# Attention: values product as high and low parts with channel-major output, probabilities divided ahead of their transposes

## The reference

```python
s = jnp.einsum('brnqhd,brnkhd->brnhqk', qb, kw).astype(jnp.float32)
s = s + bias.transpose(2, 0, 1)
...
m = jnp.max(s, axis=-1, keepdims=True)
p = jnp.exp(s - m)
den = jnp.sum(p, axis=-1, keepdims=True)
o = jnp.einsum('brnhqk,brnkhd->brnqhd', (p / den).astype(v.dtype), vw)
...
w = jax.nn.softmax(jnp.stack(lses, axis=0), axis=0)
return jnp.einsum('ibsh,ibshd->bshd', w.astype(q.dtype), jnp.stack(outs, axis=0))
...
mix = jnp.concatenate([attn, sgu], axis=-1) @ w_out
```

## Time and profile before

| | us |
|---|---|
| median of 3 runs | 1803.13 (1801.1 to 1805.96) |
| the profiled execution, time | 1803.39 |
| its span, first to last instruction | 1801.6 |
| PE busy | 1771.5 (98%) |
| DVE, ACT, POOL busy | 817.6, 652.3, 731.4 |
| attention's pairs, from the first transposes of v to the rest of the output projection | 73.3 to 221.0 |

### The profile page before, as it was taken

How to read it: one execution, slowest core, us unless ns; L and a number is a source line. 1 busy time by engine, 2 the same in 40 slices (tenths; PEclk the granted TensorE clock), 3 DMA queues, 4 the chain that set the end, 5 groups by cost and what they waited for, 6 DMA issues and landing times.

```text
span 1801.6 us, 24039 instructions
## 1 busy us (share of the span) xinstructions
PE 1771.5 (98%) x8280; PEld 1447.6 (80%) x8280; DVE 817.6 (45%) x1443; ACT 652.3 (36%) x933; POOL 731.4 (41%) x322
## 2 busy tenths in 40 slices
PE   8999999999999999999999999999999999999998
PEld 7788877888888788788888888788887788888886
DVE  4644566333333596522242244566665432422425
ACT  5544444222222333632222233454544432222323
POOL 3222235444445378244444343342423444443441
PEclk9999999999999999999999999999999999999999
DMA  8341123323222242233323233221212233232221
GB/s 221 86 99 57 47 71 105 96 97 99 94 93 94 71 123 83 70 94 117 93 82 105 93 96 102 71 83 58 82 58 70 83 105 94 82 105 93 94 92 47
DMA packets 153686, 162.28 MB, mean 90 GB/s; under 512 B 10627, under 2 KB 114679, under 8 KB 153631
## 3 DMA queue, kind: packets, MB, share of 16 engines
q1 hardware_dynamic: 149167, 158.66, 28.8%
q10 hardware_dynamic: 4464, 2.89, 0.5%
HBM read 157.84 MB, written 3.67 MB: 90 GB/s over the span
## 4 chain that ended last, share of the span: by engine, by line
PE 55%; issue 29%; POOL 10%; DVE 3%; ACT 1%; POOLq 0%; DVEq 0%; ACTq 0%
PE ps L1167 50%; POOL wlo L604 10%; PE ps L1341 2%; PE ps L1479 1%; PE ps L1330 1%; DVE ss L1697 1%; DVE acc L1719 1%; DVE h_lo L1685 0%; PE ps L1305 0%; PE ps L1306 0%; POOL wlo L611 0%; DVE xT L1722 0%; DVE sq L1878 0%; DVE xT L2187 0%; PE ps L1289 0%
## 5 line engine op out<-in xcount | busy, mean ns | idle before, releaser
L604 POOL TENSOR_TENSOR wlo<-raw,whi 128x1024 fp32r<-128x1024 f32 x256 | 617.3, 2426 | 961.2 <-ACT whi L680 947.6
L1167 PE MATMUL ps<-h_hi,wlo 128*128 128x512 f32 x1472 | 589.1, 400 | 6.3 <-POOL wlo L604 4.2
L1167 PE MATMUL ps<-h_hi,whi 128*128 128x512 f32 x1472 | 576.0, 391 | 0.0
L1167 PE MATMUL ps<-h_lo,whi 128*128 128x512 f32 x1472 | 574.9, 391 | 0.0
L680 ACT ACTIVATE whi<-raw 128x1024 fp32r<-128x1024 f32 x282 | 292.0, 1054 | 502.1 <-PE ps L1167 501.6
L1167 PEld LDWEIGHTS ps<-h_hi,wlo 128*128 128x128 f32 x1472 | 277.2, 188 | 66.6 <-issue 4.9
L1167 PE MATMUL ps<-m_hi,wlo 128*128 128x512 f32 x800 | 321.2, 401 | 3.4 <-POOL wlo L611 1.9
L1167 PEld LDWEIGHTS ps<-h_hi,whi 128*128 128x128 f32 x1472 | 276.8, 188 | 59.3
L1167 PEld LDWEIGHTS ps<-h_lo,whi 128*128 128x128 f32 x1472 | 277.4, 188 | 58.2 <-issue 3.1
L1167 PE MATMUL ps<-m_lo,whi 128*128 128x512 f32 x800 | 317.7, 397 | 0.0
L1167 PE MATMUL ps<-m_hi,whi 128*128 128x512 f32 x800 | 317.7, 397 | 0.0
(11 more groups left out here) (263 smaller groups left out, 1428.6 us busy)
## 6 DMA issues: line engine op xcount, KB each, us to landing
raw<-in_ffn_w SPq DMA_DIRECT2D x264, 256.0 KB, 2.9
raw<-in_w_ff SPq DMA_DIRECT2D x128, 256.0 KB, 2.9
raw<-in_hg_w_in SPq DMA_DIRECT2D x64, 256.0 KB, 3.2
raw<-in_w_in SPq DMA_DIRECT2D x40, 256.0 KB, 3.8
raw<-in_cp_w_in SPq DMA_DIRECT2D x24, 256.0 KB, 3.0
raw<-in_w_out SPq DMA_DIRECT2D x16, 256.0 KB, 2.9
raw<-in_cp_w_out SPq DMA_DIRECT2D x16, 256.0 KB, 3.0
raw<-in_hg_w_out SPq DMA_DIRECT2D x16, 256.0 KB, 2.9
```

Of the source, the lines that this page charges most:

```text
L604: pool.tensor_tensor(wlo[:, u % RING, :, :], raw[:, u % RING, :, :], whi[:, u % RING, :, :].bitcast(F32), ALU.subtract).then_inc(unit_lo, 1)
L1167: mm = pe.matmul(ps[:, b, :], wt[:, s, a, m * P:(m + 1) * P], xt[:, kts[a], :], start=starts and a == 0 and i == 0, stop=last)
```

## The change

The values product takes the same high and low form as the dense ones, with its output channel-major. Each block is divided by its sum in place before it is turned (DVE `scaled_weights`: a reciprocal on 128x1 and a product on 128x512). ACT makes `prob_hi` from bank 6 (`high`), DVE `prob_lo` (`turned_low`), which frees bank 6. v of a head is stationary as 128 columns: its 64 high columns and its 64 low ones (`vtok`, ACT and DVE `values_low`), and a head takes 8 matmuls of 512 columns (4 key tiles, low and high of the probabilities). The half of the output partitions that comes from v's low part is moved to the other half by ACT (`o_across`), added by DVE (`o_total`), and split by ACT `o_high` and DVE `o_low`. `onorm` and its transposes go. `values(1)` of a pair runs behind the first dense tiles of the next, and so does the transposing of v. ACT's drains of the next q and k are split by head, with `high(6)` and `high(7)` between and behind. `cuts` tells how many dense tiles stand between the steps.

```diff
+            def o_across(e, p):
+                act.wait_ge(filled[7], nth("att", ("o", e), p))
+                act.activation(o_other[own_rows(e), :], ps[own_rows(1 - e), 7, :], ACT.Copy).then_inc(o_moved, 1)
+
+            def o_high(e, p):
+                act.wait_ge(drained[7], nth("att", ("o", e), p))
+                act.activation(head_row(m_hi, e, p), head_row(osum, e, p), ACT.Copy).then_inc(o_hi, 1)
...
+                def high(i):
+                    cols = slice((i % 4) * P, (i % 4 + 1) * P)
+                    act.wait_ge(filled[6], nth("att", ("t", i), p))
+                    act.activation(prob_hi[:, :, cols], ps[:, 6, :].rearrange("p (k q) -> p k q", q=P), ACT.Copy)\
+                        .then_inc(turn_hi, 1)
...
+                high(0)
                 units(0)
-                if before_it is not None:
-                    pair_out(before_it)
-                weights(2)
                 act.wait_ge(u_cubed, 2 * p + 2)
                 act.activation(u_in[:, :], u_in[:, :], ACT.Tanh, scale=GELU_SCALE).then_inc(u_tanh, 1)
+                weights(2)
+                high(1)
...
+            def values(e, p):
+
+                pe.wait_ge(drained[6], nth("att", ("t", 4 * e + 3), p))
+                pe.wait_ge(drained[7], before("att", ("o", e), p))
+                for k in range(TT):
+                    pe.matmul(ps[:, 7, :], vtok[:, k, e, :], prob_lo[:, k, :], start=k == 0, stop=False)
+                    mm = pe.matmul(ps[:, 7, :], vtok[:, k, e, :], prob_hi[:, k, :], start=False, stop=k == TT - 1)
                 mm.then_inc(filled[7], 1)
 
-            def attend(p, units, before_it, following=None):
+            def attend(p, piece, before_it, following=None, cuts=(0, 2, 5, 7, 9, 11, 13, 15, 17, 20, 22, 24, 26, 28, 30, 32)):
...
                 def turn(i):
-                    pe.wait_ge(prob_ready, p * 8 + (i + 1))
+                    pe.wait_ge(prob_scaled, p * 8 + (i + 1))
                     pe.wait_ge(drained[6], before("att", ("t", i), p))
...
+            def scaled_weights(i, p):
+                dve.wait_ge(prob_ready, p * 8 + (i + 1))
+                dve.reciprocal(rden[:, i:i + 1], den[:, i:i + 1]).then_inc(den_inv, 1)
+                dve.wait_ge(den_inv, p * 8 + (i + 1))
+                dve.tensor_scalar(prob[:, i % 2, :], prob[:, i % 2, :], rden[:, i:i + 1], None, ALU.mult)\
+                    .then_inc(prob_scaled, 1)
+
+            def turned_low(i, p):
+                cols = slice((i % 4) * P, (i % 4 + 1) * P)
+                dve.wait_ge(turn_hi, p * 8 + (i + 1))
+                dve.tensor_tensor(prob_lo[:, :, cols], ps[:, 6, :].rearrange("p (k q) -> p k q", q=P),
+                                  prob_hi[:, :, cols].bitcast(F32), ALU.subtract).then_inc(drained[6], 1)
```

More of the change, by code:

```diff
@@ L819, in attend @@
                 act.activation(tile_of(m_hi, 4 + p), ug[:, :], ACT.Copy).then_inc(sg_hi, 1)
+                high(2)
                 units(1)
[L821 to L824, removed]
-                if following is not None:
-                    drain_qkv("qkv", following, following + 1)
+                weights(4)
+                high(3)
+                weights(5)
+                o_across(0, p)
+                units(2)
+                high(4)
+                o_high(0, p)
+                weights(6)
+                high(5)
+                units(3)
+                weights(7)
+                if following is not None:
+                    drain_head("qkv", following, following + 1, 0)
+                high(6)
+                if following is not None:
+                    drain_head("qkv", following, following + 1, 1)
+                    drain_values("qkv", following)
+                high(7)
             u_first = nth("qkv0", ("m", 3))
@@ L832, in _ @@
             attend(PAIRS - 1, u_first + PAIRS - 1, lambda i: split(U_WOUT, i) if i < 3 else None, PAIRS - 2)
-            pair_out(PAIRS - 1)
+            o_across(1, PAIRS - 1)
+            o_high(1, PAIRS - 1)
             act.preload_act_table_set(LOG_TABLES)
@@ L1331, in turn @@
                     mm.then_inc(filled[6], 1)
[L1333 to L1345, removed]
@@ L1362, in attend @@
[L1362 to L1368, removed]
+                dense(0)
+                if before_it is not None:
+                    values(1, before_it)
+                values_turned(p)
+                dense(1)
+                for i in range(4):
+                    turn(i)
+                    dense(2 + 2 * i)
+                    scores(i + 2, p)
+                    if i < 3:
+                        dense(3 + 2 * i)
@@ L1369, in attend @@
+                values(0, p)
+                dense(9)
                 turn(4)
-                units(2, second)
+                dense(10)
                 scores(6, p)
+                dense(11)
                 turn(5)
-                units(2, third)
+                dense(12)
                 scores(7, p)
-                units(3, slice(0, 6))
-                values(4)
-                values(5)
+                dense(13)
                 turn(6)
-                units(3, third)
+                dense(14)
@@ L1908, in attend @@
                 biased(2, p)
                 u_cube(p)
-                turned(1)
+                if p:
+                    o_low(1, p - 1)
+                scaled_weights(2, p)
+                turned_low(1, p)
                 biased(3, p)
                 sgu_out(p)
-                if p:
-                    pair_low(p - 1)
+                scaled_weights(3, p)
+                turned_low(2, p)
+                biased(4, p)
                 sgu_low(p)
-                turned(2)
-                biased(4, p)
@@ L1918, in attend @@
-                turned(3)
+                scaled_weights(4, p)
+                turned_low(3, p)
                 biased(5, p)
-                normal(0, p)
-                turned(4)
+                scaled_weights(5, p)
+                o_total(0, p)
+                turned_low(4, p)
                 biased(6, p)
-                turned(5)
+                o_low(0, p)
+                scaled_weights(6, p)
+                turned_low(5, p)
                 biased(7, p)
@@ L1945, in _ @@
                 attend(p)
-            pair_low(PAIRS - 1)
+            o_total(1, PAIRS - 1)
+            o_low(1, PAIRS - 1)
             logits = [vecs[:, COL["hg_lb_logits_2"] + i * HG_HEADS:COL["hg_lb_logits_2"] + (i + 1) * HG_HEADS]
```

159 lines of the change are left out of this document (81 added, 78 removed).

## The result

The changed kernel takes 1817.78 us (median of 4, 1817.66 to 1821.81), the kernel before beside it 1804.55 (1801.1 to 1806.06). The ratio is 1.0081, with a 95% interval of 1.006 to 1.0103: slower, by 13.2 us or 0.8%. The profiled execution took 1817.76 us, 14.4 more than that of before (1803.39).

A forecast was written before the change was run, and what follows sets the result against it. PE, busy 98% of the span, was taken to bound the kernel. Pairs followed through the queues sum to 157.8 us; with 2.1 and 1 more, 160.9 against 147.7 before: +13.2, so 1816 us, range 1801 to 1821.

The forecast's parts named there:

- PE's own work: PE in the attention's pairs: values matmuls and onorm transposes exchanged, 3.6 us less a pair, 14.6 in four, leaving 33.7.
- ACT and DVE: Added work in a pair: ACT +6.6 to 24.5 us, DVE +6.4 to 25.7, neither full beside PE's 33.7.
- The pair's end: PE waits before scores(0), turn(7) and the next pair's first dense tile: 0.6, 0.7 and 1.2, together 2.5 us a pair.
- POOL's hold: POOL's wlo holds DVE's u_cube and sgu_low 2.0 us each; PE waits before turn(2), turn(3), values(0): 3.7 us a pair.
- The sum: Pairs walked through the three queues: 37.1, 39.8, 39.8, 41.1; 157.8 us, with 3.1 for branches and restarts 160.9, +13.2.
- Elsewhere nothing: Outside the attention nothing moves; ACT's table load, pushed behind PE's last zv tile, is taken up by ACT's idle time.
- Not held: Rival: DVE's products and sgu_low pass beside POOL or miss it; attention 147.3 us, -0.4, kernel 1803; chance 0.20.
- All hidden: Rival: ACT and DVE run far enough ahead that all PE waits are hidden; -14.6, 1789; chance 0.06.
- The clock (1820): Rival: PE's clock falls behind the last pair's waits of 3.5 and 2.9 us; +2 to 4, 1820; chance 0.12.

The follow-up runs named there:

- the last kernel: Changed kernel with ACT's and DVE's queues and PE's cuts ordered anew, in the second order (u_cube behind scaled_weights(0), weight units later in a pair): 1788.17 us, ratio 0.9906.
- the swap of two operations: Changed kernel with ACT draining the next pair's first head ahead of the exp of block 7 instead of behind it: 1815.42 us, ratio 1.0068.
- the kernel that kept the clock up: Changed kernel with twelve small matmuls of 128 columns into unused bank 7 ahead of turn(2) of every pair: 1819.4 us, ratio 1.0084.
- the kernel with three moves: Changed kernel with u_cube ahead of turned_low(0), sgu_low behind scaled_weights(5), drain_head(0) of the next pair ahead of exp(7): 1804.67 us, ratio 0.9999.
- the kernel with POOL cut short: Changed kernel with POOL's wlo on 8 of 512 columns for 16 weight units of the attention, the other low parts left out: 1804.87 us, ratio 1.0011.
- two moves: Changed kernel with u_cube ahead of turned_low(0) and sgu_low behind scaled_weights(5), drain_head left in place: 1808.64 us, ratio 1.0025.
- the first reordered kernel: Changed kernel's operations with ACT's and DVE's queues and PE's cuts ordered anew, u_cube ahead of turned_low(0), sgu_low behind biased(7): 1797.83 us, ratio 0.9954.
- the kernel with one hold undone: Changed kernel with DVE's u_cube of each pair moved ahead of turned_low(0): 1813.55 us, ratio 1.0065.

## Why the prediction was right

It said 1816 us, +13; measured are 1817.8 and +13.2. By its steps:

- **PE's own work** (-14.6 us, 33.7 a pair). Right, and a little small. In the last kernel, where nearly every wait is gone, a pair of the loop takes 33.5 us, 4.4 less than the 37.87 for which PE was busy before, where 3.6 were forecast; the attention takes 15.4 less than before (15.8 with the transposes of v).
- **ACT and DVE.** `high` 0.589 against 0.60. The product was mis-sized: 0.487 us, not the 0.42 of the earlier trace rows, whose factor is a constant where this one is read from SBUF (whether that is the reason wasn't tried); 8 x 0.07 = 0.5 us a pair on DVE.
- **The pair's end** (0.6 + 0.7 + 1.2 = 2.5). Measured 0.62 + 0.51 + 1.17 = 2.3, and the swap of two operations changed just these.
- **POOL's hold** (1.8 before turn(2), 0.35 before turn(3), 1.5 before values(0)). The mechanism was right in every pair but the sizes were not: 2.34, 0 and 0.17. The sum of waits is 2.5 instead of 3.7, because the clock fell, which the prediction gave as a rival for the last pair alone. Some eight matmuls at 0.43 instead of 0.23 are 1.6 us more of PE work in the place of the second and third wait. In the kernel that kept the clock up the second is under 0.1, the third 1.23 and the pair as long. With the 2.34 before turn(2) that is 3.6 us, the sum that was forecast, but out of errors of 0.5, 0.3 and 0.3 that cancel: luck. The first was 0.5 us too short mainly by where PE stands. Counted from h, the start of `high(0)` at 118.47, POOL's operation runs from 1.76 to 4.17 (forecast 1.64 to 4.02) and turn(2) starts at 7.92 (7.8), but PE is there at 5.58 instead of 6.0. That `u_cube` starts 0.27 us into `wlo`, not 0.42, costs nothing, since it ends with POOL's operation either way.
- **The sum.** Pairs of 37.7, 41.1, 41.2 and 41.9 us, where the walk had 37.1, 39.8, 39.8 and 41.1, and 3.1 on top. Their sum is 161.9 against 160.9. The 3.1 had to be 4.1; in the kernel with three moves a pair of the loop takes 37.3 us with 2.66 us of waits in four places, so it takes 0.9 us beyond its 33.7 and these waits: about 0.24 us a restart. That is an estimate, but the rows point the same way: behind a wait the next matmul starts 0.34 us after the first (110.68 and 111.02 in the changed kernel), not 0.23, and the last one before it counts its full 0.40. The last pair's waits were 3.34, none, 1.99, 0.48, 1.64 and 1.38 (forecast 3.5, 1.0, 2.9, 0.75, 1.8, 1.5), again with the fallen clock in the place of the missing ones.
- **Elsewhere nothing.** Right: 1580.7 against 1580.6 us behind the attention.
- **The rivals.** Not held (1803) is near what the kernel with POOL cut short does, 1804.87, though its attention took 150.5 us and not 147.3; 1.5 of the difference is the fallen clock, and the rest wasn't followed up. The 148.9 named there follows from none of its terms; they add up to 144.2, on which its time rests. The margin of 0.4 us that was given for the hold was enough. All hidden (1789) is not what this change does, but another order of the same operations gives 1788. The argument against it, that the pair's end can't cover 7.5 us of queue, held for the order of the change only. The clock (1820) fell, in three pairs, and cost next to nothing: 161.7 us of attention with the clock kept up, against 161.9. The estimate of +2 to 4 overlooked how much of the fall is taken up by waits that would stand there anyway. Where no such wait follows, a fall did cost: 1.5 us with POOL cut short, about 1.4 with two moves.

The Trainium skill (SBUF — State Buffer, SBUF: two separate sides) calls the pair of ports that VectorE and GpSimd share an exclusive lock, on which the loser blocks fully, not a share of bandwidth. The runs agree: wherever it starts inside POOL's operation, a product ends 0.28 us behind it and the subtraction of `sgu_low` 0.55 behind it (0.42 or 0.49, and 0.69, alone). It also says that the one that starts first gets the lock. In the first reordered kernel a product that starts 0.20 us ahead of POOL takes its usual 0.48, and POOL's operation 2.55 instead of 2.40, which agrees. But the trace has the product at 130.01, POOL at 130.02, and the product waiting; a distance of 0.01 us decides nothing.

## What to carry to other kernels

Put every VectorE pass that works on SBUF alone where GpSimd is idle, or ahead of it, and count a near miss as a hit; the cheap place to look is a 0.4 us operation that takes 2.4. When a change adds work to engines that have room, follow their strict queues at the two or three places where PE is short of cover: here the loss was in the places of three operations, not in the amount of new work. A change that takes work from the bounding engine may need the whole order and the cuts made anew before the gain shows.

## What the runs showed of the hardware beyond that

Waits of the same length were followed by a fall of the clock in one place and not in another. It was at the lower level for 3.4 us or more behind each wait of 2.34 us and more before turn(2), and not behind the 1.41 us in the kernel before. Behind a wait of 2.54 us before values(0) of the last pair it fell in the kernel with one hold undone, and not in the one with the small matmuls. With POOL cut short it fell behind the 1.11 us at the end of pair 0, in the others with the same wait there it did not. So the length of the wait alone doesn't tell. A wait of 1.64 us before turn(7) of the last pair was followed by it in two kernels (the pair's end, two moves) and not in the others that have it, such as the one with three moves, in whose window at the same place the clock is 1.00:

```profile
216.80:220.20 3.40, 3.39 (x16) 2.55 (x17) 0.69 (x1) 0.60 (x1) 0.00 (x0) 1.00 0.02 5
```

DVE's operations that read PSUM ran inside POOL's `wlo` at their usual time, and so did those on one column (timelines of the first reordered kernel; POOL's operation runs from 125.83 to 128.38, and the product at 125.63 is the one that started ahead of it):

```profile
125.83 2.55 POOL L631 TENSOR_TENSOR wlo<-raw,whi 128x1024 fp32r<-128x1024 f32 x1 [4.87 <-ACT whi L707]
...
125.63 0.48 DVE L1909 TENSOR_SCALAR sq<-sq,rden 128x512 f32<-128x512 f32 x1
126.03 0.68 DVE L1938 CUSTOM_DVE_ANT_0 sq<-ps,btab 128x512 f32<-128x512 f32 x1
...
126.76 0.15 DVE L1941 TENSOR_SCALAR nmax<-amax 128x1 f32<-128x1 f32 x1
```
